# A five-layer float32 transformer on one core: weights split five chunks ahead in chunks of 1 MB, and two raw chunks in each up stage

## The reference, cut to what matters

```python
# first program, DEPTH = 4; mixer = layer % 3
for layer in range(4):
    h = rmsnorm(x, attn_norm[layer])
    m = (diff_attention, stick_breaking_attention, sliding_window_attention)[layer % 3](h, ...)
    x = x + m @ w_o[layer]                           # 1024 x 1024
    h = rmsnorm(x, ffn_norm[layer])
    u = h @ w_up                                     # 1024 x 5504, then a causal conv of width 3
    gate, val = split(conv(u) + b)
    x = x + (silu(gate) * val) @ w_down              # 2752 x 1024
x = rmsnorm(x, final_norm)
# second program, one layer
m = concat(pool_mixer(...), moba_attention(...))     # from rms_norm(x, g_mix_pre) @ w_in
x = x + rms_norm(m @ w_out, g_mix_post)
f = conv_ffn(rms_norm(x, g_ffn_pre), ...)            # 1024 x 5632, conv on the gate, gelu, 2816 x 1024
x = x + rms_norm(f, g_ffn_post)
x = x + sigmoid(x @ w_ple_gate) * (p @ w_ple)        # the gate stage
```

## Time and profile before

| | |
|---|---|
| median of the timed runs | 1572.31 us (1571.72 to 1575.10, three runs) |
| the profiled execution | 1572.28 us, its span 1570.7 us |
| busy share of the span | PE 96%, DVE 67%, ACT 55%, POOL 21% |
| chain that ended last, by engine | PE 78%, DVE 13%, ACT 6%, issue 2%, DMA 1% |
| DMA | 264.65 MB, mean 168 GB/s |
| mean granted clock of PE | 0.993 |

### The profile page before, as it was taken

The page is one execution under the profiler, slowest core; times in us unless marked ns, Lnnn a source line. Parts: engine busy times, 40 slices in busy tenths (PEclk is TensorE's granted clock), DMA queues, the critical chain, the costliest instruction groups (busy, mean ns, idle before and its releaser), DMA issues.

```text
span 1570.7 us, 31007 instructions
## 1 busy us (share of the span) xinstructions
PE 1510.8 (96%) x11560; PEld 1432.5 (91%) x11560; DVE 1048.2 (67%) x1665; ACT 863.7 (55%) x1353; POOL 325.1 (21%) x482
## 2 busy tenths in 40 slices
PE   6999999999999999989999999999999998899998
PEld 5988999899989998978999889899998887899997
DVE  5667877563378784666877576678774765766545
ACT  4666655455656564456656446666554554544533
POOL 2102222212222212212212221022212361221101
PEclk9999999999999999999999999999999998999999
DMA  6543656443336564442556545435564553455550
GB/s 251 168 154 127 210 178 228 161 171 124 134 106 203 178 233 165 161 162 82 190 184 217 184 161 174 150 131 204 175 233 158 169 161 106 148 178 194 192 205 28
DMA packets 36666, 264.65 MB, mean 168 GB/s; under 512 B 4767, under 2 KB 4826, under 8 KB 7792
## 3 DMA queue, kind: packets, MB, share of 16 engines
q1 hardware_dynamic: 33552, 255.59, 46.7%
q0 software_dynamic: 3040, 8.05, 2.0%
HBM read 262.50 MB, written 1.12 MB: 168 GB/s over the span
## 4 chain that ended last, share of the span: by engine, by line
PE 78%; DVE 13%; ACT 6%; issue 2%; DMA 1%; POOL 0%; SPq 0%; ACTq 0%; DVEq 0%
PE bank L1505 20%; PE bank L1506 19%; PE bank L1507 19%; PE bank L1516 9%; PE bank L1515 4%; DVE w_lo L817 4%; DVE tmp L870 2%; ACT w_hi L330 2%; ACT tmp L414 1%; PE bank L1550 1%; PE bank L1659 1%; DVE acc L858 1%; DVE tmp L902 1%; DVE h_lo L866 1%; DVE w_lo L826 1%
## 5 line engine op out<-in xcount | busy, mean ns | idle before, releaser
L817 DVE TENSOR_TENSOR w_lo<-w_raw,w_hi 128x2048 fp32r<-128x2048 f32 (+2 forms) x220 | 543.7, 2474 | 217.9 <-ACT w_hi L330 217.8
L1505 PE MATMUL bank<-h_hi,w_hi 128*128 128x256 f32 x2032 | 579.3, 285 | 2.7 <-DVE w_lo L817 2.7
L1506 PE MATMUL bank<-h_lo,w_hi 128*128 128x256 f32 x2032 | 574.9, 283 | 0.0
L1507 PE MATMUL bank<-h_hi,w_lo 128*128 128x256 f32 x2032 | 574.9, 283 | 0.0
L330 ACT CAST w_hi<-w_raw 128x2048 fp32r<-128x2048 f32 (+2 forms) x220 | 445.4, 2025 | 6.0 <-DMA w_raw<-w_std 3.2
L1505 PEld LDWEIGHTS bank<-h_hi,w_hi 128*128 128x128 f32 x2032 | 389.6, 192 | 8.7 <-issue 4.1
L1506 PEld LDWEIGHTS bank<-h_lo,w_hi 128*128 128x128 f32 x2032 | 389.7, 192 | 0.1
L1507 PEld LDWEIGHTS bank<-h_hi,w_lo 128*128 128x128 f32 x2032 | 389.6, 192 | 0.0
L1516 PE MATMUL bank<-act_both,w_hi 128*128 128x512 f32 x704 | 248.9, 399 | 0.0
L756 ACT ACTIVATE tmp<-bank,par 128x256 f32<-128x256 f32 x181 | 93.6, 562 | 227.1 <-PE bank L1507 226.7
L1272 DVE SCALAR_TENSOR_TENSOR tmp<-bank,par,tmp 128x255 f32<-128x255 f32 (+1 forms) x362 | 155.5, 477 | 84.8 <-ACT tmp L756 82.0
(11 more groups left out here) (180 smaller groups left out, 2000.4 us busy)
## 6 DMA issues: line engine op xcount, KB each, us to landing
w_raw<-w_std SPq DMA_DIRECT2D x181, 1024.0 KB, 4.9
w_raw<-w_down SPq DMA_DIRECT2D x40, 1408.0 KB, 6.2
act_both<-vec_dram POOLq DMA_DIRECT2D x56, 128.0 KB, 3.6
w_raw<-w_gate SPq DMA_DIRECT2D x4, 1280.0 KB, 5.4
x<-xT SPq DMA_DIRECT2D x2, 512.0 KB, 4.9
out<-x SPq DMA_DIRECT2D x4, 256.0 KB, 2.3
par<-params SPq DMA_DIRECT2D x1, 499.0 KB, 9.8
cst<-consts SPq DMA_DIRECT2D x1, 256.0 KB, 6.0
```

What stands on the lines that cost most here:

```text
L817: dve.tensor_tensor(w_lo[:, slot, 0:width], w_raw[:, slot, 0:width], w_hi[:, slot, 0:width].bitcast(F32), ALU.subtract).then_inc(lo_ready, 1)
L1505: pe.matmul(dst, wh, xh, start=first, stop=False, skip_group_check=shared)
L1506: pe.matmul(dst, wh, xl, start=False, stop=False, skip_group_check=shared)
L1507: done = pe.matmul(dst, wl, xh, start=False, stop=last, skip_group_check=shared)
```

## The change

There are now five slots (`SLOTS`) of w_hi and w_lo and three (`RAW`) of w_raw, all of 1 MB. The down weights are packed into eleven chunks of 16 tiles (`UNITS`) for each layer, and the embedding weights of the gate stage are one chunk of their own, so `weights_of` maps a chunk of the stages to one of the weights. A split is done up to a given chunk (`split_to`), and `ahead(c)` asks for the chunk five beyond c. All loops but POOL's are written out.

```diff
+SLOTS = 5
+AHEAD = 5
+RAW = 3
+        def weights_of(layer, c):
+            return c + (DOWN - DT) * layer + (layer == 5)
+        def ahead_up(j):
+            return min(AHEAD, RING + j // 3)
+        def down_weights(c0, k):
+            return FIRST_WEIGHTS[c0] + (k + 1) * FT // UNITS - 1
 # ACT (DVE the same, with hi_ready, w_lo and lo_ready)
+            def split_to(c):
+                for n in range(split[0], min(c + 1, CHUNKS)):
+                    if n >= SLOTS:
+                        act.wait_ge(used, WEIGHTS[n - SLOTS] + 1)
+                    act.wait_ge(arrived[n % RAW], n // RAW * 16 + 16)
+                    act.copy(w_hi[:, n % SLOTS, :], w_raw[:, n % RAW, :]).then_inc(hi_ready, 1)
+                    split[0] = n + 1
+            def ahead(c):
+                split_to(weights_of(layer, c) + ahead_first(layer, c))
```

In the wo stage (here DVE; ACT has `ahead(c0)` first and `ahead(c0 + 1)` between `rms` and `split_h`):

```diff
                     added_to_x(0)
-                    split_lo_halves(c0, layer)
+                    ahead(c0)
                     added_to_x(1)
                     added_to_x(2)
-                    next_split(c0, 1)
...
                         raw_low(app, 7)
-                        next_split(c0, 2)
                         normalise(app, SUMS[name][2])
-                        next_split(c0, 3)
+                        ahead(c0 + 1)
```

In the down stage on both engines, with `postponed_splits` gone from the next stage:

```diff
-                        if k < DT - 1:
-                            next_split(c0, k)
+                        split_to(down_weights(c0, k) + AHEAD)
...
-                        postponed.append((c0, DT - 1))
```

In the up stage the first two chunks are raw, and the statistic is in the second; their results are scaled by rstd, the first one's at the head of `normalise`, the second one's in step 1:

```diff
+            def scaled_up(c, j):
+                dve.wait_ge(used, c + 1)
+                for v, bank in enumerate((pj, val_bank)):
+                    dve.tensor_tensor(u_sb[:, 2 * j + v, :], bank[c % RING][:, 0:S], rstd[:, :],
+                                      ALU.mult).then_inc(first_scaled, 1)
             def normalise(app, norm):
                 dve.wait_ge(rstd_done, norm + 1)
+                if raw_chunks(app) == 2:
+                    scaled_up(first_chunk[app], 0)
...
 # PE
+                    for k in range(3):
+                        slot = slot_of(c0, k)
+                        pair(c0 + k, (pj[slot][:, 0:S], val_bank[slot][:, 0:S]), app, shared=False,
+                             raw=prev if k < 2 else None, last=k == 1)
```

```diff
+                    for k in range(4):
+                        embedding(k)
...
+                        if k == n - 1:
+                            outputs(weights, 0, pj[slot][:, 0:S]).then_inc(gate_half, 1)
+                            outputs(weights, 1, ov[:, 0:S]).then_inc(used, 1)
+                            continue
```

More of the change, by code:

```diff
@@ L281, in _ @@
         def _(sp):
-            for n in range(2):
+            for n, parts in enumerate(((0, 1), (2,))):
                 a, b = n * DT // 2, (n + 1) * DT // 2
                 sp.dma_start(x[:, a:b, :], xT[:, a:b, :]).then_inc(x_in[n], 16)
[L285 to L318, removed]
@@ L325, in _ @@
+            for n, (a, b) in enumerate(OUT_TILES):
+                sp.wait_ge(out_ready, n + 1)
+                sp.dma_start(out[:, a:b, :], x[:, a:b, :]).then_inc(stored, 16)
+            sp.wait_ge(stored, 16 * len(OUT_TILES))
         @block.scalar
         def _(act):
[L327 to L339, removed]
@@ L467, in _ @@
             squares("x", 0)
+            act.wait_ge(norms_in, 16)
+            raw_high(0, 0)
+            first_split(0)
+            raw_high(0, 1)
+            first_split(1)
+            raw_high(0, 2)
+            raw_high(0, 3)
             squares("x", 1)
             act.wait_ge(x_in[1], 16)
[L470 to L478, removed]
+            raw_high(0, 4)
+            squares("x", 2)
+            first_split(2)
+            raw_high(0, 5)
+            squares("x", 3)
+            squares("x", 4)
+            raw_high(0, 6)
+            raw_high(0, 7)
+            for t in range(3):
+                act.wait_ge(vec_psum, t + 1)
+                act.copy(vec_copy(t), banks[3 + t][0:16, 0:NVEC]).then_inc(vec_sb, 1)
+            split_to(2)
             half = s_half = d_half = b_half = ffn = app = 0
@@ L1584, in project_half @@
                     chunk_ready(c)
-                done = outputs(slot, tile, pj[slot][:, tile * S:tile * S + S])
+                done = outputs(weight_slot(layer, c), tile, pj[slot][:, tile * S:tile * S + S])
                 if tile:
@@ L1854, in _ @@
                     sb_scores(0, 1)
-                    with pe.Fori(0, 3) as i:
+                    for i in range(3):
                         group(i, True)
@@ L1943, in _ @@
[L1943 to L1947 removed]
+                        slot, weights = slot_of(c0, k), weight_slot(layer, c0 + k)
+                        outputs(weights, 0, pj[slot][:, 0:S])
+                        outputs(weights, 1, val_bank[slot][:, 0:S]).then_inc(used, 1)
@@ L1958, in down @@
                         if a == 0:
-                            chunk_ready(c)
-                        weights = [w_tile(slot, k, P, 0) for k in range(a, b)]
+                            pe.wait_ge(bank_free, c0 + f + 1)
+                        bank = pj[slot_of(c0, f)]
+                        weights = [down_tile(f, k) for k in range(a, b)]
                         if layer < 4:
```

570 lines of the change are left out of this document (279 added, 291 removed).

## The result

The changed kernel takes 1601.64 us (median of four runs, 1600.86 to 1603.37) against 1573.4 us for the one before, run beside it (1571.72 to 1575.1): 1.0185 times as long, 95% interval 1.0173 to 1.0198. Its profiled execution took 1601.47 us (span 1599.8 us, mean granted clock 0.980 against 0.993), the forecast was 1601.

What follows compares the result with a forecast made beforehand. PE was taken as the bound, movable only at stage changes, start and end. Terms -4.7 + 11.7 - 2.8 + 12.9 + 3.1 - 1.3 + 10.2 = +29.1 on 1572.28 gave 1601 us; own range 1596 to 1607, overall 1581 to 1614.

Steps and rivals of the forecast that it cites:

- the start: Start of the kernel: third chunk begins at 28.6 instead of 33.32 us, a gain taken as 4.7 us.
- the mixer: Mixer stage after a down stage: splits ahead of normalise make the third chunk later, 1250.15 against 1247.75, +2.4 us.
- wo to up, layers 0 to 3: Change from wo to up: stall before the third up chunk grows from 0.7 to 6.5 us, +2.9 each, +11.7.
- the clock's 1.7: After six stalls (five up stages, the gate) PE restarts at half rate, 1.7 us each, +10.2 us.
- down to attention, layers 1 to 3: After down stages: two splits ahead of rms and normalise make the third attention chunk later, +3.5 us per layer.
- the 1.3 for w_lo waits: Window and mixer stages: other waits for w_lo disappear with the lead of five, -1.3 us.
- The fifth layer's up and down: Layer 4, wo to up: a w_lo and its wait leave the post-norm additions, -2.8 us before any clock cost.
- The gate: Gate stage: two w_lo ahead of p_lo delay the embedding from 1535.01 to 1540.8; with a shorter tail, +3.1 us.
- Rivals 1 and 4: First: queue order costs no stall, 1545 us, chance 0.09. Second: nearly neutral, gains against half the stalls, 1572 us, 0.03.
- Rival 2: The stalls come but the clock stays: 1591 us, chance 0.22.
- rival 3: The clock takes 3.1 us at six stalls and 1 at four, +22.6 instead of 10.2: 1614 us, chance 0.17.
- Rival 5: Later up chunks wait for w_lo too, DVE not catching up: 2.3 us more in five stages, 1612 us, chance 0.04.

Runs made afterwards that it cites:

- E4: Kernel after, with 12 extra throwaway matmuls on TensorE during the wait for the third up chunk, five up stages: 1591.19 us.
- E1: Kernel after, with the third up chunk's weight split moved ahead of root mean square (ScalarE) and of normalise (VectorE), all five layers: 1582.93 us.
- E2: Kernel after, with the eighth down tile's two splits put behind root mean square and normalise (in the gate stage behind add_normed): 1592.13 us.
- E8: E7, with only one of ScalarE's two postponed splits ahead of the high parts of the attention's input, the other behind them: 1558.74 us.
- E6: Kernel after, with layer 0's attention three chunks ahead all through instead of going up to five: 1600.47 us.
- E7: E3, with the fourth up chunk's split also moved, behind normalise (ScalarE: ahead of the high parts): 1569.04 us.
- E9: E8, with TensorE's fourth and fifth up chunk waiting for scaled copies of the first two chunks' banks instead of their convolutions: 1557.74 us.
- E12: E9 plus E10's edit, the statistic at the end of the first raw chunk: 1553.05 us.
- E10: E8, with the sums of squares added up at the end of the first raw chunk instead of two tiles into the second: 1553.09 us.
- E13: Kernel after, with only the statistic moved, to the end of the first raw chunk: 1599.11 us.
- E3: Kernel after, with both the third up chunk's split early and the eighth down tile's splits late: 1571.47 us, ratio 0.9994.

## Why the prediction was right

The total was right to 0.2 us, which is closer than its parts: the mechanism held in the up stages, after the down stages and at the gate, but two terms, the start and the mixer, missed by 3.4 and 3.9 us in opposite ways. That they cancel is luck. Where two figures stand, the first is the forecast.

- **wo to up, layers 0 to 3**: 4 x (2.9 + 1.7) = 18.4, measured 18.40. Here too two small misses cancel: the wait's own part was 2.9 against 2.5 to 2.7, the clock's 1.7 against 1.95 (E4), and 1.7 was chosen as the nearer of two rows, with single stages at 1.34 to 2.69. The stall was forecast at 6.5 us and is 6.44 to 6.45 from matmul to matmul. E1 shows the cause: with the third split moved ahead of the normalisation (and of rms on ACT) and nothing else changed, the stall is gone.
- **down to attention, layers 1 to 3**: 10.5 against 9.46. Allowing for the 4.06 us behind, rstd ends 333.2 (forecast 333.4) and the normalisation starts 335.1 (335.2). I forecast no clock loss here, though the trace has one stretch of 3.4 us of half rate in each of these stages (the kernel before has one in layer 2's); what it cost was not separated. E2 and E8 together show the cause.
- **The mixer** is a term whose path I had wrong: 2.4, less some of the 1.3 for w_lo waits, against -1.46. I took the last squares to come when they did before. There DVE had a split ahead of the last addition to x, and PE then waited 2.23 us for ACT's squares. With the down weights in eleven chunks that split comes earlier (at 1228.5, allowing for the 26.53 us that the kernel after is behind), the wait is gone, and the normalisation starts 1.75 us later than before instead of 4.5. The third chunk starts 0.35 us earlier than before instead of 2.4 later. The first two rows are the kernel before, the last one the kernel after.
```profile
1231.27 2.29 DVE L817 TENSOR_TENSOR w_lo<-w_raw,w_hi 128x2048 fp32r<-128x2048 f32 x1 [1.11 <-ACT w_hi L330]
1235.25 0.70 PE L1627 MATMUL bank<-sq,cst 128*128 128x512 f32 x1 [2.23 <-ACT sq L362]
...
1265.66 1.67 DVE L886 SCALAR_TENSOR_TENSOR tmp<-x,both_gains,rstd 128x256 f32<-128x256 f32 x4
```
- **The fifth layer's up and down**: -2.8 + 1.7 = -1.1 against -0.61; of this the clock is 2.64 (E4), so the rest is -3.25.
- **The gate**: 3.1 + 1.7 = 4.8 against 4.7. The embedding was to be 5.8 us later and is 5.8 later.
- **The start** is a term that was mis-sized: -4.7 against -1.33. The third chunk came as forecast (28.6 against 27.98, a gain of 5.3), but 4 us were given back within the same attention stage, in three waits for ScalarE's copies that the forecast did not have. E6 shows that the extra splits of layer 0 (five ahead, caught up at its fourth and seventh chunk) make two of them.
- **Rivals.** Rivals 1 and 4 fall by the stalls themselves. Rival 2 (no clock cost) falls by E4, rival 3 (3.1 each) too. Rival 5 (ACT and DVE don't catch up) did not occur in the kernel after, where no up stage has a wait behind the third chunk. But something like it occurs as soon as the stall is taken away: 2.84 us at the fourth chunk for w_lo (E1), 2.39 there for a convolution (E7), 2.05 at the fifth for w_lo (E9), 1.3 there with the statistic early (E12).
- **The statistic.** I took its place as a given, at a cost of 1.3 us a stage. E10 and E13 show that 1.4 us a stage of delay were avoidable: the wait for the sums was a matter of six tiles, and the change puts the statistic off by eight.

Still open: how much the half rate in the attention stages costs, why the attention and the mixer lost 5 us in E1, and what makes a wait of 2.4 us lose the clock in one execution and not in another.

## What to carry over

Before splitting work further ahead, list for each queue what it now stands in front of: here a split of 1.9 to 2.8 us cost nothing in an idle stretch of about 5 us before rstd (E1), and left behind the normalisation it held TensorE for 6.4 us in each of five stages. When a wait is taken away, look one chunk further at once, since the next late operation sets what is left: E3 only drew level, and the three small moves after it (E7, E8, E10) brought 18 us. Place a reduction where its inputs are just ready, no later. And check the parts of a sum that came out right.

## What the runs showed of the hardware

Twelve useless matmuls in each of five waits of 6.4 us made the kernel 10 us faster, since the real ones behind them ran at full rate (28 against 15 in the same 3.4 us). Whether a wait of 2.4 to 2.8 us is followed by half rate varied: of the four up stages in layers 0 to 3, two had 3.4 us of it in E1 and four in E3 (waits of 2.84 us), three in E7 and none in E8 (waits of 2.38 and 2.39 us). In the kernel after the clock fell within the wait already (a mean of 0.68 over layer 0's), and behind the waits of layers 0 to 3, all of 6.44 or 6.45 us, the half rate lasted 3.2 to 6.2 us more.
